# A two-block network on one core: the second expert table for 192 tokens as stationary blocks, for the last 64 tokens as gathered rows

## The chip, the core and the metric

The kernel runs on one core of a Trainium2 chip. The number that counts is the device time of one execution, in microseconds; the median of the runs is given. The engines are TensorE (PE, with its weight loads as PEld), VectorE (DVE), ScalarE (ACT), GpSimd (POOL) and SyncE (SP, which only issues DMAs here).

## What is computed

256 tokens of width 1024 go through two blocks: a block with an mLSTM mixer, an MLP and a gated embedding, then a block with two mixers and, at its end, an expert layer. Only this last layer is touched. Its reference, cut to what matters:

```python
q = (xb @ w_q).reshape(t, 8, 2, 128)
s = einsum('thpd,hpkd->thpk', q, sub_keys)
top_s, top_i = lax.top_k(s, 16)
cand_s = top_s[:, :, 0, :, None] + top_s[:, :, 1, None, :]
cand_i = top_i[:, :, 0, :, None] * 128 + top_i[:, :, 1, None, :]
best_s, best_pos = lax.top_k(cand_s.reshape(t, 8, 256), 16)
idx = take_along_axis(cand_i.reshape(t, 8, 256), best_pos, axis=-1)
gate = softmax(best_s, axis=-1)
h = gelu(einsum('thkd,td->thk', u_table[idx], xb))
y = einsum('thk,thkd->td', gate * h, v_table[idx])
x = layer_norm(DN_ALPHA * x + y)
```

Each token chooses 8 x 16 = 128 of 16384 experts; `u_table` and `v_table` have a row of 1024 for each.

## The kernel before

**Weights as a stream.** All weights are a list of 438 items of 128 x 1024 fp32 (512 KB). An item goes through a ring of four slots: SP loads it to `RAW` (wait `w_lo` of the item four before), ScalarE casts it to the high half `WH` (fp32r; waits `w_landed` and `w_used` of the item four before, counts `w_hi`), GpSimd or VectorE subtracts `RAW - WH` to the low half `WL` (counts `w_lo`), TensorE multiplies with high and low halves and counts `w_used`. A product is split in three: high x high, high x low, low x high.

**First table (`u`, 128 items).** No rows are chosen: for each item j, TensorE computes the products of 128 experts with all 256 tokens (24 matmuls of 256 columns, table blocks stationary), ScalarE applies gelu into `HS[:, j, :]` (128 partitions x 256 tokens). Low halves are GpSimd's (`split_low`, L398-L403). A round of four items is `u_body`.

**Gates.** VectorE finds the chosen experts; from `HOT_AT` = 15 on, one block of 16 tokens for each round, it writes one-hot rows (`one_hots`), TensorE turns them into a 128 x 128 table of gates for each token (`gates_of`, L1643), and VectorE multiplies the part j < `KEPT` = 60 into `HS` (`gate`). The rest is parked in DRAM (`gates_rest`) through `stage` and multiplied in during the second table (`fetch` on ScalarE's queue, `gate_rest` on VectorE).

**Second table (`v`, 128 items).** For item j, `HS[:, j, :]`, now gated, is the stationary operand, as high half `CH` (ScalarE, `c_high`) and low half `CL` (VectorE, `c_low`), and the table block with 1024 columns is moved past it: for both tiles of 128 tokens and both halves of 512 columns, three matmuls, so 12 of 512 columns (`v_item`, L1694). The sums stay in four banks of PSUM, tokens on the partitions. VectorE makes both low halves (`v_low`, `c_low`); GpSimd has nothing to do. The last four items are taken tile by tile, so that the first tile's layer norm runs beside the second tile's matmuls. All orders are written out in the code; every engine works through its own instructions strictly in that order.

## Time and profile before

| | us |
|---|---|
| median of 3 runs | 1406.85 |
| the 3 runs | 1406.48 to 1407.96 |
| span of the profiled execution | 1407.2 |

| engine | busy, us | share of the span |
|---|---|---|
| TensorE | 1379.8 | 98% |
| TensorE, weight loads | 1219.1 | 87% |
| VectorE | 889.0 | 63% |
| ScalarE | 869.5 | 62% |
| GpSimd | 763.7 | 54% |

The page gives the profiled execution by its span, from the first to the last instruction; it is 0.35 us above the median of the runs. The span falls into stages: up to about 690 us everything ahead of the tables, then the first table (with the gates in it from 829 us), the second table from 1051.47 us, and a last norm from 1399.85 us. Shares over the whole span mix these stages, so they are read one by one below. Busy times of matmuls overlap, since a matmul starts before the one ahead has drained; what a matmul costs is read from start to start.

### The profile page before, as it was taken

Reading aid. Unit: us, or ns where it says so; the run is one execution under the profiler, and the core shown is the slowest. Engines: PE = TensorE matmul, PEld = TensorE weight load, DVE = VectorE, ACT = ScalarE, POOL = GpSimd, SP = SyncE. Lnnn points to the kernel's source line nnn. Section 1 sums busy time; section 2 is a strip of 40 time slices with the busy share of each in tenths; the row PEclk is TensorE's granted clock in tenths of the full one; section 3 lists DMA queues with packets and bytes.
Section 4 is the critical chain, followed back from the end, with each engine's and each line's share of the span. In section 5 each row is a group of like instructions: output and inputs, shape, how many; then the busy total and the mean of one; then the engine's idle time right before and its main releaser. Section 6 shows DMA issues by size and latency. Waiting matters only on the chain.

```text
span 1407.2 us, 28597 instructions
## 1 busy us (share of the span) xinstructions
PE 1379.8 (98%) x9422; PEld 1219.1 (87%) x9422; DVE 889.0 (63%) x1967; ACT 869.5 (62%) x1496; POOL 763.7 (54%) x350
## 2 busy tenths in 40 slices
PE   7999999999999999899999999999999999999997
PEld 6878888887998777789999999999998888888886
DVE  3674883114764654535997059999977766655555
ACT  5475775446855656566666768888874444445553
POOL 6885889886776424687888877777740000000000
PEclk9999999999999999999999999999999999999999
DMA  5633566655453312655555556565669777666552
GB/s 199 204 133 120 183 194 199 188 194 165 147 163 125 122 61 85 199 195 165 190 173 190 180 174 201 196 202 191 201 200 324 272 241 241 210 194 193 192 192 94
DMA packets 75352, 256.63 MB, mean 182 GB/s; under 512 B 8472, under 2 KB 8856, under 8 KB 75032
## 3 DMA queue, kind: packets, MB, share of 16 engines
q1 hardware_dynamic: 64192, 231.76, 50.3%
q10 hardware_dynamic: 11096, 24.00, 5.0%
q8 instruction: 42, 0.69, 0.2%
q14 instruction: 22, 0.18, 0.1%
HBM read 244.72 MB, written 11.01 MB: 182 GB/s over the span
## 4 chain that ended last, share of the span: by engine, by line
PE 75%; POOL 12%; issue 8%; DVE 3%; DMA 1%; ACT 0%; POOLq 0%; ACTq 0%; DVEq 0%; SPq 0%
PE PS L1080 64%; POOL WL L402 11%; PE PS L1125 2%; PE PS L1643 2%; PE PS L1126 1%; PE PS L1462 1%; DMA RAW<-weights 0%; PE PS L1420 0%; DVE MINV L2167 0%; DVE GA L1810 0%; DMA fbias<-fox_bias 0%; DVE XS L2277 0%; DVE GA L1809 0%; PE PS L1619 0%; PE PS L1364 0%
## 5 line engine op out<-in xcount | busy, mean ns | idle before, releaser
L402 POOL TENSOR_TENSOR WL<-RAW,WH 128x1024 fp32r<-128x1024 f32 x306 | 739.4, 2427 | 270.5 <-ACT WH L461 182.6
L1080 PE MATMUL PS<-XHL,WH 128*128 128x256 f32 x2528 | 460.7, 284 | 2.4 <-DVE XHL L1763 1.5
L954 ACT CAST WH<-RAW 128x1024 fp32r<-128x1024 f32 x252 | 263.9, 1047 | 226.2 <-PE PS L1080 212.9
L1080 PEld LDWEIGHTS PS<-XHL,WH 128*128 128x128 f32 x2528 | 394.4, 192 | 5.9 <-issue 3.4
L1080 PE MATMUL PS<-XHL,WL 128*128 128x256 f32 x1264 | 357.7, 283 | 0.0
L461 ACT CAST WH<-RAW 128x1024 fp32r<-128x1024 f32 x184 | 191.3, 1047 | 108.9 <-PE PS L1080 95.8
L1080 PEld LDWEIGHTS PS<-XHL,WL 128*128 128x128 f32 x1264 | 242.6, 192 | 0.0
L2447 DVE TENSOR_TENSOR WL<-RAW,WH 128x1024 fp32r<-128x1024 f32 x128 | 156.6, 1224 | 116.9 <-ACT WH L954 116.2
L1080 PE MATMUL PS<-WH,CH 128*128 128x512 f32 x512 | 199.2, 389 | 0.0
L1080 PE MATMUL PS<-WL,CH 128*128 128x512 f32 x512 | 199.2, 389 | 0.0
L1080 PE MATMUL PS<-WH,CL 128*128 128x512 f32 x512 | 199.2, 389 | 0.0
L1125 PE MATMUL PS<-XHL,WH 128*128 128x512 f32 x384 | 138.3, 403 | 0.5 <-DVE XHL L2291 0.4
L1080 PE MATMUL PS<-WH,XHL 128*128 128x512 f32 x352 | 119.2, 403 | 1.2 <-POOL WL L402 1.2
L1080 PEld LDWEIGHTS PS<-WL,CH 128*128 128x128 f32 x512 | 96.1, 188 | 20.1
L1080 PEld LDWEIGHTS PS<-WH,CL 128*128 128x128 f32 x512 | 96.1, 188 | 19.9
L1080 PEld LDWEIGHTS PS<-WH,CH 128*128 128x128 f32 x512 | 96.1, 188 | 19.8
L930 ACT ACTIVATE hot_j<-hot_j,GQ 128x128 fp32r<-128x128 f32 x256 | 89.2, 395 | 33.7 <-DVE hot_j L2397 33.7
L1126 PE MATMUL PS<-XHL,WL 128*128 128x256 f32 x384 | 108.0, 281 | 0.0
L2397 DVE TENSOR_SCALAR hot_j<-PS,JT,GH 128x128 fp32r<-128x128 f32 x256 | 92.1, 401 | 0.0
L1125 PEld LDWEIGHTS PS<-XHL,WH 128*128 128x128 f32 x384 | 72.7, 189 | 18.2 <-issue 1.2
L1080 PEld LDWEIGHTS PS<-WH,XHL 128*128 128x128 f32 x352 | 66.6, 189 | 17.6 <-ACT og L579 1.2
L1126 PEld LDWEIGHTS PS<-XHL,WL 128*128 128x128 f32 x384 | 73.1, 190 | 0.0
(407 smaller groups left out, 1959.3 us busy)
## 6 DMA issues: line engine op xcount, KB each, us to landing
RAW<-weights SPq DMA_DIRECT2D x438, 512.0 KB, 3.5
gates_rest<-stage ACTq DMA_DIRECT2D x32, 272.0 KB, 2.2
stage<-gates_rest ACTq DMA_DIRECT2D x32, 272.0 KB, 4.2
H<-x SPq DMA_DIRECT2D x2, 512.0 KB, 4.7
LG<-rows ACTq DMA_DIRECT2D x2, 512.0 KB, 6.6
LB<-rows ACTq DMA_DIRECT2D x2, 512.0 KB, 8.9
x<-H ACTq DMA_DIRECT2D x1, 1024.0 KB, 6.1
HY<-x ACTq DMA_DIRECT2D x1, 1024.0 KB, 13.2
```

What stands on the lines that cost most here:

```text
L402: nc.gpsimd.tensor_tensor(WL[:, slot, :], RAW[:, slot, :], plain(WH[:, slot, :]), ALU.subtract).then_inc(w_lo, 1)
L461: nc.scalar.copy(high_of(n), RAW[:, slot, :]).then_inc(w_hi, 1)
L930: last = A(hot_j[:, g, a, 1, :], plain(hot_j[:, g, a, 0, :]), ACT.Copy, scale=at_token(GQ, t))
L954: nc.scalar.copy(WH[:, slot, :], RAW[:, slot, :]).then_inc(w_hi, 1)
L1080: last = mm(dst, a, b, start=start and k == 0, stop=stop and k == len(pairs) - 1)
L1125: mm(both, wh, XHL[:, :, k, :], start=(k == 0), stop=False)
L1126: last = mm(PS[:, bank, 0:S], wl, XH[:, k, :], start=False, stop=(k == KC - 1))
L1462: last = mm(product_of(half, h2, crossed)[:, u * CH_T:(u + 1) * CH_T], inv[a][rows, unit, :], right, start=True, stop=True)
L1643: last = mm(PS[:, 4 + 2 * (c % 2) + g, a * 2 * NK:(a + 1) * 2 * NK], hot_i[:, g, a, :], hot_j[:, g, a, :, :], start=True, stop=True)
L2397: last = V.tensor_scalar(hot_j[:, g, a, 0, :], iota_ps, at_token(JT, t + a), at_token(plain(GH), t + a), ALU.is_equal, ALU.mult)
L2447: V.tensor_tensor(WL[:, slot, :], RAW[:, slot, :], plain(WH[:, slot, :]), ALU.subtract).then_inc(w_lo, 1)
```

## The change

Of the 256 tokens, the last `TS` = 64 leave the dense way through the second table. `TD` = 192 stay in it.

- **192 tokens, table blocks stationary.** High and low halves of the gated hidden values stand side by side in `CHL` (2 x 192). For each of 8 chunks of 128 output columns, the high half of the table block is loaded and 384 columns (high and low) are moved past it, then the low half of the block, past which 192 are moved. The result has output columns on the partitions, one PSUM bank for each chunk. At the end ScalarE and VectorE add the two parts of a bank, and TensorE transposes back (`back`).
- **64 tokens, rows gathered.** For 64 steps, GpSimd gathers 128 rows of 1024 from the second table (`gather_row`, two experts of each of the 64 tokens, three buffers `rows_v`) and 128 hidden values (`gather_hidden`) by indirect DMA; VectorE multiplies each row by gate and hidden value and adds it up in `sparse_y` (`add_row`). TensorE folds the two groups of 64 partitions (`sparse_back`). The hidden values of these tokens are stored to DRAM (`hidden`) during the first table, by SP after each round, the last by ScalarE.
- **Low halves.** Every fourth low half of the second table is GpSimd's (`value_low`, counting `pool_lo`), three of four are VectorE's.
- **Gates** are made for 12 blocks of 16 tokens and not 16, so `HOT_AT` is 19; `KEPT` is 64.
- **The end.** The last four items are taken chunk by chunk once all four are ready; both tiles' norms come after them.
- **Semaphores** of earlier stages are used again (`LATER` maps a name to an old one and its last value), and the loops over the second table are written out without a loop on ScalarE, VectorE and GpSimd.

The diff, cut to its core:

```diff
-IJG_AT = NK // 8 - 2
-HOT_AT = NK // 8 - 1
-HOT_END = HOT_AT + S // 16
-KEPT = 4 * HOT_AT
+IJG_AT = NK // 8 - 2
+HOT_END = NK // 4 - 1
+HOT_AT = HOT_END - TD // 16
+KEPT = 64
+MAC_FROM, MAC_TO = 13, 119
+MAC_AT = [MAC_FROM + k * (MAC_TO - MAC_FROM) // STEPS for k in range(STEPS)]
+BATCH = STEPS // 8
...
 @block.gpsimd
+            def value_low(j):
+                slot = (V0 + j) % RING
+                pool.wait_ge(w_hi, V0 + j + 1)
+                nc.gpsimd.tensor_tensor(WL[:, slot, :], RAW[:, slot, :], plain(WH[:, slot, :]),
+                                        ALU.subtract).then_inc(sem("pool_lo"), 1)
+            def gather_row(k):
+                if k >= ROWS:
+                    pool.wait_ge(sem("row_added"), late_at("row_added", k - ROWS + 1))
+                nc.gpsimd.indirect_dma_start(
+                    out=rows_v[:, k % ROWS, :], out_offset=None, in_=expert_rows,
+                    in_offset=bass.IndirectOffsetOnAxis(ap=v_row[:, k:k + 1], axis=0)).then_inc(
+                        sem(f"row_landed{k % ROWS}"), 16)
...
+            for k in range(ROWS):
+                gather_row(k)
+            for q in range(NK // RING):
+                value_low(RING * q + RING - 1)
+                if q == 0:
+                    pool.wait_ge(sem("h_stored"), late_at("h_stored", 16 * (SELF_STORED + 1)))
+                for k in range(STEPS):
+                    if max(MAC_AT[k] - 20, 0) // RING == q:
...
+                        gather_hidden(k)
+                for k in range(STEPS):
+                    if MAC_AT[k] // RING == q and k + ROWS < STEPS:
+                        gather_row(k + ROWS)
...
 @block.tensor
-            def v_item(j, c, start=False, stop=False, tiles=range(NT)):
...
-                    for half in range(2):
-                        wh = WH[:, slot, half * 512:(half + 1) * 512]
-                        wl = WL[:, slot, half * 512:(half + 1) * 512]
-                        last = split([(h, wh), (h, wl), (l, wh)], PS[:, 2 * t + half, :], start, stop)
+            def v_chunk(c, ch, start=False, stop=False):
+                slot = (V0 + c) % RING
+                wh, wl = WH[:, slot, ch * P:(ch + 1) * P], WL[:, slot, ch * P:(ch + 1) * P]
+                mm(PS[:, ch, 0:2 * TD], wh, CHL[c][:, :, :].rearrange("p a t -> p (a t)"), start=start, stop=False)
+                return mm(PS[:, ch, 0:TD], wl, CHL[c][:, 0, :], start=False, stop=stop)
...
+            for c in range(RING):
+                item_ready(NK // 4 - 1, c)
...
+            for ch in range(KC):
+                for c in range(RING):
+                    last = v_chunk(c, ch, stop=(c == RING - 1))
+                last.then_inc(sem("chunk_done"), 1)
+                if ch >= 3:
+                    back(ch - 3)
...
 @block.vector
+            def add_row(k):
...
+                wait(f"row_landed{k % ROWS}", 16 * (k // ROWS + 1))
+                wait("row_added", late_at("row_added", k))
...
+                    V.scalar_tensor_tensor(sparse_y[:, :], rows_v[:, k % ROWS, :], h_s[:, k:k + 1], sparse_y[:, :],
+                                           ALU.mult, ALU.add).then_inc(sem("row_added"), 1)
...
+            for j in range(NK):
+                if j % RING < RING - 1:
+                    value_low(j)
+                c_low(j)
...
+                if rests < TD // 16 and (j in (5, 7, 9, 11) or j > 12 and j % RING == 1):
+                    for b in range(2):
+                        gate_rest(rests, b)
+                    rests += 1
+                for k in range(STEPS):
+                    if MAC_AT[k] == j:
+                        add_row(k)
...
-                layer_norm(1, t, [2 * t, 2 * t + 1], DN_ALPHA, LG2, LB2, 64, "y_ready")
+                layer_norm(1, t, [t, 2 + t], DN_ALPHA, LG2, LB2, 64, "y_ready")
```

What this does to the order of instructions. On VectorE, in the loop over the second table while parked gates are still fetched, before (`WL` is a low half, `CL` a remainder, `HS<-HS,stage` a gate multiply):

```order
L2447 TENSOR_TENSOR WL<-RAW,WH 128x1024 [waits w_hi]
L2424 REGISTER_ALU
L2426 ISA [waits ch_ready]
L2426 TENSOR_TENSOR CL_183<-HS,CH 128x256
L2418 ISA
L2420 ISA [waits fetched0]
L2420 TENSOR_TENSOR HS<-HS,stage 128x68x8
L2420 ISA [waits fetched1]
```

The same place now (items 17 to 19; `sparse_y` is the running sum of rows, and the semaphore named `s_ready` counts the adds):

```order
L2626 TENSOR_TENSOR WL<-RAW,WH 128x1024 [waits w_hi]
L2602 TENSOR_TENSOR CHL_186<-HS,CHL_186 128x192 [waits ch_ready]
L2597 TENSOR_TENSOR HS<-HS,stage 128x64x8 [waits fetched0]
L2597 TENSOR_TENSOR HS<-HS,stage 128x64x8 [waits fetched1]
L2640 SCALAR_TENSOR_TENSOR sparse_y<-rows_v,h_s,sparse_y 128x1024 [waits s_ready,row_landed0]
L2626 TENSOR_TENSOR WL<-RAW,WH 128x1024 [waits w_hi]
L2602 TENSOR_TENSOR CHL_187<-HS,CHL_187 128x192 [waits ch_ready]
L2602 TENSOR_TENSOR CHL_188<-HS,CHL_188 128x192 [waits ch_ready]
L2640 SCALAR_TENSOR_TENSOR sparse_y<-rows_v,h_s,sparse_y 128x1024 [waits s_ready,row_landed1]
```

Row adds stand among the low halves, and the fourth item of a round has a remainder but no low half. On GpSimd, the end of the program before (the last low halves of the first table, with nothing behind them):

```order
L402 TENSOR_TENSOR WL<-RAW,WH 128x1024 [waits w_hi]
L445 REGISTER_ALU
L445 COMPARE_AND_BRANCH
L402 TENSOR_TENSOR WL<-RAW,WH 128x1024 [waits w_hi] x2
L118 UNCONDITIONAL_BRANCH
```

And now, three rounds of four items in the second table (`rows_v` is a gather of rows, `h_s` one of hidden values):

```order
L529 TENSOR_TENSOR WL<-RAW,WH 128x1024 [waits w_hi]
L543 DMA h_s<-hidden,h_at 128x1 x2
L536 DMA rows_v<-weights,v_row 128x1024 [waits s_ready] x2
L529 TENSOR_TENSOR WL<-RAW,WH 128x1024 [waits w_hi]
L543 DMA h_s<-hidden,h_at 128x1 x2
L543 DMA h_s<-hidden,h_at 128x1 [waits s_ready]
L536 DMA rows_v<-weights,v_row 128x1024 [waits s_ready] x3
```

GpSimd goes on through the second table, with one low half and some five gathers for each round, each row gather behind an add of VectorE.

## Rows read from the trace of the kernel before

**Rows 1.** The page's busy line: busy us, share of the span, instructions.

```profile
PE 1379.8 (98%) x9422; PEld 1219.1 (87%) x9422; DVE 889.0 (63%) x1967; ACT 869.5 (62%) x1496; POOL 763.7 (54%) x350
```

**Rows 2.** Stages: length, busy by engine (instructions), granted clock, DMA share, GB/s.

```profile
829.15:1051.47 222.32, 222.32 (x1854) 222.13 (x1852) 208.64 (x573) 185.51 (x419) 153.99 (x64) 1.00 0.59 196
1051.47:1399.85 348.38, 348.35 (x1538) 288.20 (x1536) 221.07 (x296) 172.94 (x257) 0.00 (x0) 1.00 0.65 217
```

**Rows 3.** Chain of waits, late gates and second table: start, length, engine and line.

```profile
1034.35 0.48 PE PS L1643 x4
1034.83 2.88 PE PS L1080 x24
...
1041.55 358.28 PE PS L1080 x1620
```

**Rows 4.** Timeline of TensorE at key scores: start, length, line, names, weights, columns.

```profile
604.62 0.28 PE L1619 MATMUL PS<-KK,QH 128*128 128x256 f32 x1
604.74 0.23 PE L1620 MATMUL PS<-KK,QL 128*128 128x128 f32 x1
604.80 0.34 PE L1619 MATMUL PS<-KK,QH 128*128 128x256 f32 x1
604.98 0.22 PE L1620 MATMUL PS<-KK,QL 128*128 128x128 f32 x1
605.03 0.44 PE L1125 MATMUL PS<-XHL,WH 128*128 128x512 f32 x1
605.32 0.28 PE L1126 MATMUL PS<-XHL,WL 128*128 128x256 f32 x1
```

**Rows 5.** Timeline of ScalarE and VectorE in the second table, where VectorE is behind.

```profile
1083.10 1.05 ACT L954 CAST WH<-RAW 128x1024 fp32r<-128x1024 f32 x1
...
1084.40 1.39 DVE L2420 TENSOR_TENSOR HS<-HS,stage 128x544 f32 x2
1085.71 1.22 DVE L2447 TENSOR_TENSOR WL<-RAW,WH 128x1024 fp32r<-128x1024 f32 x1
1086.85 0.42 DVE L2426 TENSOR_TENSOR CL<-HS,CH 128x256 fp32r<-128x256 f32 x1
1087.18 1.22 DVE L2447 TENSOR_TENSOR WL<-RAW,WH 128x1024 fp32r<-128x1024 f32 x1
```

**Rows 6.** Timelines of GpSimd and VectorE, early; one line's shortest, median, longest ns.

```profile
149.78 2.41 POOL L402 TENSOR_TENSOR WL<-RAW,WH 128x1024 fp32r<-128x1024 f32 x1 [0.26 <-ACT WH L461]
...
150.53 0.42 DVE L1936 SCALAR_TENSOR_TENSOR RT<-PS,RB 128x256 f32<-128x256 f32 x1
150.87 1.59 DVE L1928 TENSOR_TENSOR ZL<-ZF,ZH 128x256 fp32r<-128x256 f32 x1
...
L1928 DVE TENSOR_TENSOR ZL<-ZF,ZH x32: 409/1578/1595, 142.9 to 226.8; 128x256 fp32r<-128x256 f32 x32
...
675.18 2.28 DVE L2344 TENSOR_TENSOR cand<-tv 128x2048 f32<-128x2048 f32 x1
...
675.59 6.51 POOL L402 TENSOR_TENSOR WL<-RAW,WH 128x1024 fp32r<-128x1024 f32 x2 [0.47 <-ACT WH L954]
```

**Rows 7.** Two short windows (columns as rows 2); DMA issues from 1060 to 1100.

```profile
1060.00:1070.00 10.00, 10.00 (x46) 8.29 (x45) 4.95 (x7) 4.06 (x6) 0.00 (x0) 1.00 1.02 414
1080.00:1090.00 10.00, 10.00 (x45) 8.28 (x45) 9.75 (x14) 5.45 (x9) 0.00 (x0) 1.00 0.92 285
...
RAW<-weights SPq DMA_DIRECT2D x14, 512.0 KB, 5.0
```

**Rows 8.** Timeline of the last norm on VectorE; six fp32 transposes in the chain.

```profile
1399.85 0.69 DVE L2270 SCALAR_TENSOR_TENSOR HY<-HY,PS 128x512 f32<-128x512 f32 x1 [0.47 <-PE PS L1080]
...
1401.44 1.28 DVE L2277 SCALAR_TENSOR_TENSOR XS<-HY,ST,LG 128x1024 f32<-128x1024 f32 x1
...
1403.34 1.42 DVE L2283 SCALAR_TENSOR_TENSOR HY<-XS,ST,LB 128x512 f32<-128x512 f32 x2
...
812.66 0.66 PE PS L1681 x6
```

More of the change, by code:

```diff
@@ L286, in sem @@
         def sem(name):
+            name = LATER[name][0] if name in LATER else name
             if name not in sems:
@@ L1040, in _ @@
[L1040 to L1043 removed]
+                if j >= 12 and j % RING == 0 and j // RING <= TD // 16 - 2:
+                    next_blocks(j // RING)
+                if j == 40:
+                    act.wait_ge(w_used, V0 + 32)
+                    act.wait_ge(sem("x2_stored"), 16)
+                    act.dma_start(LG2[:, :], rows_in[4:5, :].broadcast_to([P, D])).then_inc(sem("ln_landed"), 16)
+                    act.dma_start(LB2[:, :], rows_in[5:6, :].broadcast_to([P, D])).then_inc(sem("ln_landed"), 16)
+                    act.dma_start(HY[:, :, :].rearrange("p t d -> p (t d)"), x2_dram).then_inc(sem("x2_back"), 16)
@@ new lines, in _ @@
+            wait("u_bank_free", NK // 2)
+            for ch in range(2):
+                last = v_chunk(0, ch, start=True)
+            last.then_inc(w_used, 1)
+            for c in range(1, RING):
+                item_ready(0, c)
+                for ch in range(KC):
+                    last = v_chunk(c, ch)
+                last.then_inc(w_used, 1)
+            with pe.Fori(1, NK // 4 - 1) as i:
+                for c in range(RING):
+                    item_ready(i, c)
+                    for ch in range(KC):
+                        last = v_chunk(c, ch)
+                    last.then_inc(w_used, 1)
@@ new lines, in _, with back @@
+            for c in range(RING):
+                item_ready(NK // 4 - 1, c)
+            def back(ch):
+                wait("units_ready", late_at("units_ready", 1))
+                wait("chunk_summed", late_at("chunk_summed", max(ch + 1, 2 if ch < 4 else 4)))
+                g, k = ch // 4, slice(ch % 4 * P, ch % 4 * P + P)
+                first_tile = tp(PS[:, 2 * g, k], dense_y[:, ch, 0:P], unit[:, :])
+                second_tile = mm(PS[0:TD - P, 2 * g + 1, k], dense_y[:, ch, P:TD], unit[:, :], start=True, stop=True)
+                if ch == KC - 1:
+                    first_tile.then_inc(sem("tile_done"), 1)
+                    second_tile.then_inc(sem("tile_done"), 1)
@@ new lines, in sparse_back @@
+            def sparse_back(g):
+                wait("row_added", late_at("row_added", STEPS))
+                wait("chunk_summed", late_at("chunk_summed", 2 * g + 2))
+                mm(PS[P - TS:P, 2 * g + 1, :], group_sum[:, :], sparse_y[:, g * 512:(g + 1) * 512], start=True, stop=True)
+            for ch in range(KC):
+                for c in range(RING):
+                    last = v_chunk(c, ch, stop=(c == RING - 1))
+                last.then_inc(sem("chunk_done"), 1)
+                if ch >= 3:
+                    back(ch - 3)
+                if ch in (4, 6):
+                    sparse_back(ch // 2 - 2)
@@ L1720, in _ @@
+            for ch in range(KC - 3, KC):
+                back(ch)
         @block.vector
@@ L2440, in _ @@
                     gate(i, c - 1)
-            gate(S // 16 - 1, 3)
-            def v_low(j, c):
-                slot = (FIRST["v_table"] + c) % RING
-                dve.wait_ge(w_hi, j + (FIRST["v_table"] + 1))
-                V.tensor_tensor(WL[:, slot, :], RAW[:, slot, :], plain(WH[:, slot, :]), ALU.subtract).then_inc(w_lo, 1)
-            dve.wait_ge(w_lo, FIRST["v_table"])
-            for c in range(4):
-                v_low(c, c)
-                c_low(c, c)
-            wait("u_bank_free", NK // 2)
@@ L2473, in _, with value_low @@
-            for c in range(4):
-                low_halves(KEPT + c, c)
-            with dve.Fori(HOT_AT + 1, NK // 4) as i:
-                for c in range(4):
-                    v_low(4 * i + c, c)
-                    c_low(4 * i + c, c)
+            gate(TD // 16 - 1, 3)
+            V0 = FIRST["v_table"]
+            def value_low(j):
+                slot = (V0 + j) % RING
+                dve.wait_ge(w_hi, V0 + j + 1)
+                V.tensor_tensor(WL[:, slot, :], RAW[:, slot, :], plain(WH[:, slot, :]), ALU.subtract).then_inc(w_lo, 1)
@@ L2480, in _ @@
+            assert rests == TD // 16
+            for ch in range(KC):
+                wait("y_low_ready", late_at("y_low_ready", ch + 1))
+                V.tensor_tensor(dense_y[:, ch, :], PS[:, ch, 0:TD], y_low[:, ch % 2, :], ALU.add).then_inc(
+                    sem("chunk_summed"), 1)
             wait("x2_back", 16)
```

300 lines of the change are left out of this document (186 added, 114 removed).

## Prediction, made before the changed kernel ran

> **What bounds the kernel now.** I read the busy line first, then the table by stage, the chain, and last single instructions. TensorE is busy 98% of the span [rows 1], and in the three stages of the expert tables it has no gap at all, at a granted clock of 1.00 [rows 2]. The chain of waits agrees: from the end of the gates to 1399.83 us it is one unbroken piece of matmuls [rows 3]. So time is won there only by giving TensorE less to do, and only as long as the engines that feed it keep the new pace. The second-table stage (1051.47 to 1399.85, 348.4 us) is 1536 matmuls of 512 columns, 0.227 us each, 12 to a block: 2.72 us for each of the 128 blocks. Beside them VectorE is busy 221 us, ScalarE 173 us, GpSimd 0, and the DMA share is 0.65 [rows 2].
>
> **TensorE in the second table.** A block now takes, for each of 8 chunks, one matmul of 384 and one of 192 columns: 4608 columns, not 6144. Price of a matmul: 512 columns start 0.23 us apart (348.4/1536 = 0.227) and 256 columns 0.12 us (24 in 2.88 us) [rows 2, 3], so 0.107 us for each 256 columns and 0.013 us fixed. By that line 384 columns cost 0.174 and 192 cost 0.094 us: 8 x 0.268 = 2.14 us a block. The nearest rows to the short one speak against the line. Two pairs of 256 and 128 columns and then one of 512 take from 604.62 to 605.32, 0.70 us; less 2 x 0.12 and 0.235, the two of 128 columns cost 0.225, so 0.112 us each instead of the 0.067 of the line [rows 4]. Something of about 0.11 us between two loads of weights seems to be a floor. With 0.112 for the 192 columns a block is 8 x 0.286 = 2.29 us, and I take that. 128 blocks: 274 us by the line, 293 by the floor, against 348.
>
> The Trainium skill, TensorE: Matmul & The Clock Gate, "Back-to-back issue gap", gives about 81 ns for 128 columns in a stream of load and matmul pairs. The rows here show 112 ns for such a matmul, so the measurement decides; by the page's figure, as an estimate, there would be no floor at 192 columns, and the TensorE term would be the 274 us.
>
> **The gates in the first table.** Only 192 tokens get one-hot matmuls, so 12 of the 16 blocks of gates stay (HOT_AT moves from 15 to 19). One block is 4 groups of 0.48 us on a full TensorE [rows 3]: 4 blocks x 4 x 0.48 = 7.7 us saved. VectorE has 208.6 of 222.3 us in that stretch [rows 2]; its work for each block hardly changes (64 blocks kept in place rather than 60), so nothing new is late. The stores of the last 64 tokens' hidden values stand on SP behind loads that it has issued by then, and wait for evacuations some ten blocks old: nothing.
>
> **VectorE and GpSimd in the second table: the new limit.** The order lists show for each four blocks on VectorE three low halves, four coefficient remainders and two or three row adds, on GpSimd the fourth low half and some five gathers. Prices by start-to-start [rows 5]: a low half 1.14 us (1085.71 to 1086.85), a remainder of 256 columns 0.33 (1086.85 to 1087.18), so 0.27 for 192; a pair of gate multiplies of 544 1.31 (1084.40 to 1085.71), so 1.24 for a pair of 512. A row add is a scalar_tensor_tensor of 1024, which the trace has at 1.28 us [rows 8] where the low half has 1.22, so 1.20 start-to-start; the small multiplies of the gates come to 1 us in all. VectorE alone: 96 x 1.14 + 128 x 0.27 + 64 x 1.20 + 12 x 1.24 + 1 = 237 us, 1.85 us a block. By this alone TensorE would stay the bound.
>
> But the two engines do not run side by side on this work. At 150.87 VectorE starts ZL<-ZF,ZH, 256 columns with both inputs in SBUF, while GpSimd is inside a low half (149.78 for 2.41 us); it takes 1.59 us instead of 0.41 at its shortest and ends 0.27 us after GpSimd. RT<-PS,RB just before, with one input in PSUM, takes its 0.42 us inside the same GpSimd instruction. The other way round, GpSimd's low half of 675.59 has to sit out VectorE's 2.28 us: two of them take 6.51 us together [rows 6]. So a VectorE instruction with both inputs in SBUF and a GpSimd low half exclude one another. Before, GpSimd was idle in this stage; now 32 low halves of 2.4 us run there, and every VectorE instruction of the stage has both inputs in SBUF. The two add: 237 + 32 x 2.4 = 314 us. The quarter that was given to GpSimd thus costs VectorE 2.4 us a piece, where doing it itself would cost 1.14.
>
> Now in order of time, T0 being TensorE's first block. Blocks 0 to 12 have no adds: 13 x (0.86 + 0.27 + 0.6) + 5 pairs x 1.24 = 29 us on VectorE and GpSimd, 13 x 2.29 = 30 on TensorE: TensorE's pace, and VectorE, three blocks ahead, reaches block 13 at about T0 + 24. Blocks 13 to 118: 106 x 1.73 + 64 x 1.20 + 7 x 1.24 = 269 us, 2.53 us a block, above TensorE's 2.29. Where VectorE was behind in the trace it was busy 9.75 of 10 us [rows 7], so 276 us: T0 + 300. Then TensorE's pace for 6 blocks, 14 us. The last four blocks start only when all four low halves are there: after block 123 a cast (1.05 us [rows 5]) and GpSimd's 2.4 us: 3.5 us with TensorE idle, where the old code went on block by block. Then 4 x 2.29 = 9 us, and the transposes back: 16 at 0.11 us (0.66 us for 6 fp32 transposes [rows 8]) and two sums of 512 columns at four times that, 2.6 us; they are at most that, and nothing if they fit beside other waits. Sum: T0 + 329 instead of 348: **19 us saved**.
>
> **The end.** Both tiles' layer norms now come after the last matmul; before, the first ran beside the second tile's matmuls. One norm goes from 1399.85 to 1404.76, 4.9 us [rows 8]. The second adds these 4.9, and copy, add and transposes of the last chunk some 1.3: **6 us lost**.
>
> **Gathers.** The trace has no indirect DMA. 128 of them stand on GpSimd, half of 512 KB and half of 0.5 KB. No row is near; for the issue I take as the lower end nothing and as the upper end GpSimd's longest common instruction, one low half, 2.4 us. In 9.9 us (four blocks) GpSimd has 3.0 us for its low half with a wait, and 4.9 gathers: it fits up to 1.4 us each. I take about 1 us, so hidden, and keep both ends. The Trainium skill, DMA: Bandwidth & Descriptors, "Latency and other measured facts", puts about 1 us before the first byte of a DMA generated on GpSimd; at that estimate the 128 would be 128 us of GpSimd, and the sum would not change. No run shows it yet.
>
> **The sum.** 1407.2 (span) - 7.7 - 19 + 6 = 1386.5; the median lies 0.35 us under the span, so **1386 us**. Own range 1372 (no floor at 192 columns, no idle in VectorE's queue) to 1400 (a few us at the start, where the first four row gathers and the wait for the stores precede GpSimd's first low halves).
>
> **Rivals.** (a) *TensorE stays the bound*: the exclusion does not bite, because the low half on GpSimd slips into VectorE's gaps. Then 274 to 293 us of matmuls + 3.5 + 2.6: 280 to 299, so 49 to 68 saved in the stage, 1337 to 1357. For it: the remaining VectorE load of 1.85 us a block. Against: VectorE has no gaps long enough, by the sum above.
>
> (b) *The DMA engines saturate.* The stage moves 67 MB of table and now 34 MB of gathered rows and 6 MB of gates, 107 MB. At 414 GB/s, the best ten microseconds (share 1.02), that is 258 us and hidden; at 285 GB/s for a share of 0.92 [rows 7], 310 at full share, it is 345 us, as long as the stage was. Then the stage gains nothing but the gates' 7.7 us are kept and the end's 6 are lost: 1395 to 1415, about no change. 4 KB rows from random places are read like the table's rows, which speaks against the worse figure.
>
> (c) *Rows arrive late, and it becomes slower.* A row's gather stands on GpSimd behind the low half of its group, and that waits for a cast, which waits for TensorE to give the slot free. Take the row for block 21: block 15 on TensorE 2.3, cast 1.2, GpSimd's low half 3.0, two small gathers and one large, then the landing, 5 us in the busiest stretch [rows 7]; VectorE comes to block 21 six blocks after block 15, 15 us later. So three issues have 3.7 us, 1.2 each; beyond that VectorE waits in its queue with low halves behind the add, and TensorE behind them. At 2 us an issue it is 2.3 us late in each of some 26 groups, +60 us: 1446. The point where the gain is gone: 21 us / 26 groups, 0.8 us late in each, an issue of 1.5 us. For it: three buffers of rows and a strictly ordered queue. Also here: GpSimd holding the port while it makes descriptors, 64 x 1 us or more.
>
> **Chances.** Forecast 0.48, (a) 0.12, (b) 0.14, (c) 0.26. Faster by over 0.2% (about 3 us, what a measurement of this kernel can tell from no change): 0.47 + 0.12 + 0.05 = 0.64; within 0.2%: 0.01 + 0.04 + 0.02 = 0.07; slower: 0.05 + 0.24 = 0.29. The range leaves out the low end of (a) and the upper part of (c): 1345 to 1450.
>
> **What would show it.** In the changed kernel's profile: pairs of 384 and 192 columns 0.27 to 0.29 us apart; VectorE close to 100% in blocks 13 to 118, its low halves stretched to some 3 us about once in four blocks; TensorE's waits there ending with VectorE's or GpSimd's low half; a gap of about 3.5 us ahead of the last four blocks; two norms in a row at the end. Rival (a): no TensorE gap before the last group. (b): ScalarE's casts waiting for RAW. (c): row adds waiting for the gather. It is wrong if the low halves on GpSimd do not stretch VectorE's instructions, or if a gather holds GpSimd for longer than 1.4 us.

## Result: slower, and the profile after

The median is 1441.51 us (1440.85 to 1453.14) against 1406.66 us for the kernel before: a ratio of 1.0263 (95% interval 1.0246 to 1.0280), 35 us slower. The forecast was 1386 us; the time lies inside the range, on the other side of no change, near rival (c). The busy line of the profiled execution (span 1439.9 us; engine, us, share, instructions) answers to [rows 1]:

```profile
PE 1351.2 (94%) x9898; PEld 1241.8 (86%) x9898; DVE 914.6 (64%) x1870; ACT 837.8 (58%) x1424; POOL 999.9 (69%) x516
```

TensorE's share fell from 98% to 94% although it has less to do. The table by stage (stretch, length, busy time and instructions of PE, PEld, DVE, ACT and POOL, granted clock, DMA share, GB/s) answers to [rows 2]; the second table now begins at 1041.1 us, and the transposes back follow its last matmul at 1425.2:

```profile
829.15:1041.05 211.90, 211.75 (x1754) 210.73 (x1753) 159.52 (x435) 158.57 (x339) 150.01 (x63) 1.00 0.63 200
1041.05:1426.90 385.85, 329.20 (x2075) 320.81 (x2074) 286.28 (x326) 166.12 (x261) 235.73 (x164) 0.91 0.78 278
```

The first line is what was hoped for: TensorE full, 10.4 us gained by the fewer gates. The second is the loss: 386 us where the stage before had 348. No engine is full in it, VectorE has 286 of 386 us, and the granted clock is 0.91 where it was 1.00, since TensorE now stops again and again. What each waited for, 1045 to 1405 us (engine, line and tile, releaser; us in total, times, longest):

```profile
ACT WH L1106 <- DMA RAW<-weights: 115.4, 49, 8.0
POOL WL L529 <- ACT WH L1106: 84.9, 24, 10.2
ACT WH L1106 <- PE PS L1831: 79.4, 52, 6.3
DVE sparse_y L2640 <- DMA rows_v<-weights,v_row: 55.0, 20, 7.6
PEld PS L1830 <- DVE CHL L2602: 53.2, 19, 6.7
```

Everybody waits for everybody: ScalarE for weights and for TensorE, GpSimd for ScalarE, TensorE for VectorE. Only the fourth line is new in kind: the row adds wait for gathered rows. GpSimd's groups in 1045 to 1385 us (line, engine, operation, tiles, count; busy us, mean ns; idle before):

```profile
L543 POOL DMA_INDIRECT h_s<-hidden,h_at x64 | 77.4, 1209 | 15.7 <-issue 13.9
L536 POOL DMA_INDIRECT rows_v<-weights,v_row x63 | 75.3, 1196 | 23.5 <-issue 15.6 <-DVE sparse_y L2640 7.4
L529 POOL TENSOR_TENSOR WL<-RAW,WH 128x1024 fp32r<-128x1024 f32 x30 | 74.9, 2497 | 74.8 <-ACT WH L1106 74.7
```

A gather holds GpSimd for 1.2 us on the mean, a small one as long as a large one, and 0.3 us lie between two in a row: 1.5 us. Over all 127 of these two lines, with the idle time put down to "issue", it is 1.43 us each. The Trainium skill, DMA: Bandwidth & Descriptors, "Latency and other measured facts", has about 1 us to the first byte of such a DMA. No row here shows a first byte; for GpSimd's own time the measured 1.5 us decides. Now one wait in order of time, first GpSimd, then VectorE (start, us, instruction; idle before it and what ended it):

```profile
1176.44 2.39 POOL L529 TENSOR_TENSOR WL<-RAW,WH 128x1024 fp32r<-128x1024 f32 x1 [2.23 <-ACT WH L1106]
1178.99 1.77 POOL L543 DMA_INDIRECT h_s<-hidden,h_at  x1
1181.07 1.38 POOL L543 DMA_INDIRECT h_s<-hidden,h_at  x1 [0.30 <-issue]
1182.75 1.09 POOL L543 DMA_INDIRECT h_s<-hidden,h_at  x1 [0.30 <-issue]
1184.15 1.10 POOL L536 DMA_INDIRECT rows_v<-weights,v_row  x1 [0.30 <-issue]
```
```profile
1170.99 1.27 DVE L2640 SCALAR_TENSOR_TENSOR sparse_y<-rows_v,h_s,sparse_y 128x1024 f32<-128x1024 f32 x1
...
1176.45 3.47 DVE L2640 SCALAR_TENSOR_TENSOR sparse_y<-rows_v,h_s,sparse_y 128x1024 f32<-128x1024 f32 x1 [0.94 <-DMA rows_v<-weights,v_row]
...
1184.08 0.35 DVE L2602 TENSOR_TENSOR CHL<-HS,CHL 128x192 fp32r<-128x192 f32 x1
1191.08 1.28 DVE L2640 SCALAR_TENSOR_TENSOR sparse_y<-rows_v,h_s,sparse_y 128x1024 f32<-128x1024 f32 x1 [6.65 <-DMA rows_v<-weights,v_row]
```

The cast ended at 1176.37. Behind it stand the low half, three gathers of hidden values, and only at 1184.15 the row that VectorE wants: it lands near 1191, and for 6.65 us VectorE stands with all later low halves behind the add. The buffer for that row had long been free: the add three rows earlier (1170.99) ended at 1172.26, so its gather started 11.9 us late. Over all rows a gather starts a mean of 4.9 us after its buffer is free (start of each row's gather less the end of the add three rows before, from the two timelines).

Rows land a median 7.4 us after their issue, and weights now take 6.2 us and not 3.5 (lines of the DMA issues; the kernel before over its whole span, where its second table alone has 3.5 too, then the changed kernel, 1070 to 1380 us):

```profile
RAW<-weights SPq DMA_DIRECT2D x438, 512.0 KB, 3.5
```
```profile
RAW<-weights SPq DMA_DIRECT2D x105, 512.0 KB, 6.2
rows_v<-weights,v_row POOLq DMA_INDIRECT x61, 7.4
```

### The profile page after: what moved, and what is told of

Read it like the earlier page. It is cut to its first block, busy times and chain, and to the rows that moved or that the text cites. A ratio compares the mean times of both kernels' runs of the same rounds, so it can differ in the third digit from the quotient of the medians.

```text
span 1439.9 us, 28703 instructions
## 1 busy us (share of the span) xinstructions
PE 1351.2 (94%) x9898; PEld 1241.8 (86%) x9898; DVE 914.6 (64%) x1870; ACT 837.8 (58%) x1424; POOL 999.9 (69%) x516
## 4 chain that ended last, share of the span: by engine, by line
PE 55%; POOL 16%; issue 10%; DMA 8%; DVE 8%; ACT 2%; ACTq 0%; POOLq 0%; DVEq 0%; SPq 0%
PE PS L1204 37%; POOL WL L472 11%; PE PS L1830 5%; DMA rows_v<-weights,v_row 5%; POOL WL L529 2%; PE PS L1249 2%; POOL h_s L543 2%; PE PS L1831 2%; DMA RAW<-weights 2%; PE PS L1767 2%; DVE sparse_y L2640 1%; ACT WH L1106 1%; DMA stage<-gates_rest 1%; PE PS L1250 1%; PE PS L1586 1%
## 5 line engine op out<-in xcount | busy, mean ns | idle before, releaser
L472 POOL TENSOR_TENSOR WL<-RAW,WH 128x1024 fp32r<-128x1024 f32 x306 | 739.5, 2427 | 259.5 <-ACT WH L583 177.9
L1830 PE MATMUL PS<-CHL,WH 128*128 128x384 f32 x1024 | 322.3, 384 | 56.7 <-DVE CHL L2602 52.7
L1831 PE MATMUL PS<-CHL,WL 128*128 128x192 f32 x1024 | 267.8, 262 | 0.0
L1830 PEld LDWEIGHTS PS<-CHL,WH 128*128 128x128 f32 x1024 | 207.6, 203 | 63.7 <-DVE CHL L2602 53.2
L1106 ACT CAST WH<-RAW 128x1024 fp32r<-128x1024 f32 x128 | 134.4, 1050 | 206.8 <-DMA RAW<-weights 115.4
L1204 PEld LDWEIGHTS PS<-XHL,WL 128*128 128x128 f32 x1264 | 242.4, 192 | 0.0
L1831 PEld LDWEIGHTS PS<-CHL,WL 128*128 128x128 f32 x1024 | 210.8, 206 | 0.0
L529 POOL TENSOR_TENSOR WL<-RAW,WH 128x1024 fp32r<-128x1024 f32 x32 | 79.6, 2489 | 91.7 <-ACT WH L1106 91.6
L2640 DVE SCALAR_TENSOR_TENSOR sparse_y<-rows_v,h_s,sparse_y 128x1024 f32<-128x1024 f32 x63 | 91.8, 1458 | 63.8 <-DMA rows_v<-weights,v_row 55.0
L2626 DVE TENSOR_TENSOR WL<-RAW,WH 128x1024 fp32r<-128x1024 f32 x96 | 122.7, 1278 | 9.7 <-ACT WH L1106 8.8
L536 POOL DMA_INDIRECT rows_v<-weights,v_row x64 | 76.9, 1201 | 31.7 <-issue 15.6
L543 POOL DMA_INDIRECT h_s<-hidden,h_at x64 | 77.4, 1209 | 15.7 <-issue 13.9
```

The lines of the kernel that those rows point to most:

```text
L472: nc.gpsimd.tensor_tensor(WL[:, slot, :], RAW[:, slot, :], plain(WH[:, slot, :]), ALU.subtract).then_inc(w_lo, 1)
L529: nc.gpsimd.tensor_tensor(WL[:, slot, :], RAW[:, slot, :], plain(WH[:, slot, :]), ALU.subtract).then_inc(sem("pool_lo"), 1)
L1106: nc.scalar.copy(WH[:, slot, :], RAW[:, slot, :]).then_inc(w_hi, 1)
L1204: last = mm(dst, a, b, start=start and k == 0, stop=stop and k == len(pairs) - 1)
L1830: mm(PS[:, ch, 0:2 * TD], wh, CHL[c][:, :, :].rearrange("p a t -> p (a t)"), start=start, stop=False)
L1831: return mm(PS[:, ch, 0:TD], wl, CHL[c][:, 0, :], start=False, stop=stop)
```

## The experiments

The expectations speak of four theories. **Theory 1**: the rows' traffic makes weights late, and a ring of four slots can't hide that. **Theory 2**: the exclusion of GpSimd's low halves and VectorE alone sets the pace (the forecast's own mechanism, larger than I had it). **Theory 3**: rows are late because their gather stands in GpSimd's queue behind a low half, so behind a cast, and behind small gathers (rival (c)). **Theory 4**, found on the way: VectorE's unbroken runs hold up the gathers. All runs, in the order of the text, against the kernel before:

| run | us | ratio, 95% interval |
|---|---|---|
| changed kernel | 1441.5 | 1.0263 (1.0246 to 1.0280) |
| a_short_rows | 1427.2 | 1.0144 (1.0127 to 1.0162) |
| b_dve_lows | 1422.6 | 1.0094 (1.0059 to 1.0129) |
| c_both | 1402.1 | 0.9969 (0.9950 to 0.9989) |
| d_short_adds | 1419.2 | 1.0073 (1.0053 to 1.0094) |
| h_no_gathers | 1387.1 | 0.9857 (0.9836 to 0.9879) |
| e_early | 1392.4 | 0.9895 (0.9871 to 0.9918) |
| f_stt | 1391.5 | 0.9889 (0.9867 to 0.9910) |
| g_seven | 1388.4 | 0.9855 (0.9831 to 0.9879) |
| k_ahead | 1413.4 | 1.0045 (1.0027 to 1.0063) |
| n_ahead_short | 1415.6 | 1.0051 (1.0031 to 1.0072) |
| p_no_hidden | 1426.5 | 1.0135 (1.0118 to 1.0153) |
| j_early_short | 1385.3 | 0.9845 (0.9828 to 0.9861) |
| l_tuned | 1379.5 | 0.9801 (0.9755 to 0.9846) |
| m_tuned32 | 1386.2 | 0.9848 (0.9831 to 0.9864) |

**a_short_rows.** Row gathers fetch 64 bytes of 4096.

```diff
-                    out=rows_v[:, k % ROWS, :], out_offset=None, in_=expert_rows,
+                    out=rows_v[:, k % ROWS, 0:D if k < ROWS else 16], out_offset=None, in_=expert_rows if k < ROWS else short_rows,
...
```

> All from the changed kernel; from the fourth gather on only 16 of the 1024 columns of each gathered row are fetched (the rest of the buffer keeps older rows, so the sums of the last 64 tokens are not those of the reference). Number of gathers, their issues, waits and the row adds stay: only some 32 MB of row traffic are gone. Theory 1, the rows' traffic makes the weights late (landing of a weight item 6.2 us instead of 3.5, in a ring of four slots): landing of RAW back to 3.4 to 3.8 us, ScalarE's waits for RAW (115 us) below 30 us, and the time falls by 40 us or more, to 1380 to 1400, where the sum of VectorE and GpSimd's low halves would set the pace. Theory 2, GpSimd's low halves and VectorE's instructions exclude each other and that alone sets the pace: 1430 to 1442, almost nothing. Theory 3, the gathers are issued too late behind GpSimd's other work: the issues stay, so most of the 55 us of row adds waiting stays, 1420 to 1440.

1427.2 us. Weights landed in 3.8 us again and the row gathers in 4.0, yet only 14 us came back, much as the third theory said: in this order of GpSimd's queue the traffic is not the main thing.

**b_dve_lows.** VectorE makes every low half.

```diff
-                nc.gpsimd.tensor_tensor(WL[:, slot, :], RAW[:, slot, :], plain(WH[:, slot, :]),
-                                        ALU.subtract).then_inc(sem("pool_lo"), 1)
...
-                if j % RING < RING - 1:
-                    value_low(j)
+                value_low(j)
```

> All from the changed kernel; the fourth low half of each four blocks is made by VectorE in the same place, GpSimd keeps its wait and its gathers. Theory 1 (weights late by the rows' traffic): the way of a slot from landing to free is 1.2 us shorter for one slot in four, and the traffic stays: 1415 to 1435, with RAW still landing after 6 us. Theory 2 (exclusion sets the pace): VectorE has 32 x 1.14 us more and loses 32 x 2.4 us of exclusion, so about 40 us less, 1390 to 1405 or lower. Theory 3 (late gathers): GpSimd has 77 us more for gathers, so the rows come earlier, 1400 to 1420.

1422.6 us, 19 us less: inside theory 1's span, just above theory 3's, and theory 2 is missed. The exclusion is gone (remainders are back at a mean of 352 ns, from 518), but the row adds still wait 51 us for their gathers, which stand behind the wait for the cast that GpSimd keeps.

```profile
L2639 DVE SCALAR_TENSOR_TENSOR sparse_y<-rows_v,h_s,sparse_y 128x1024 f32<-128x1024 f32 x63 | 80.8, 1283 | 54.8 <-DMA rows_v<-weights,v_row 51.0
```

**c_both.** Both edits.

> Both edits at once: 16 columns of each gathered row (from the fourth gather on; the last 64 tokens' sums are not the reference's) and all low halves on VectorE. Nothing is left but TensorE's 2.29 us a block if the two causes are all there is: stage of 293 us plus the end, 1345 to 1360. If the small gathers' issue (1.4 us each, start to start) or VectorE's 273 us with its waits is still late: 1360 to 1390.

1402.1 us, worse than every expectation. With no traffic and no exclusion, row adds still wait 34.8 us for gathered rows. So neither was the core of it. Some gathers last three times as long as others; GpSimd, then VectorE in the same stretch:

```profile
1134.19 2.51 POOL L542 DMA_INDIRECT h_s<-hidden,h_at  x1 [2.96 <-ACT WH L1105]
1137.00 3.70 POOL L542 DMA_INDIRECT h_s<-hidden,h_at  x1 [0.30 <-issue]
```
```profile
1137.00 1.22 DVE L2626 TENSOR_TENSOR WL<-RAW,WH 128x1024 fp32r<-128x1024 f32 x1
1138.13 0.35 DVE L2602 TENSOR_TENSOR CHL<-HS,CHL 128x192 fp32r<-128x192 f32 x1
1138.40 1.21 DVE L2626 TENSOR_TENSOR WL<-RAW,WH 128x1024 fp32r<-128x1024 f32 x1
1139.54 0.35 DVE L2602 TENSOR_TENSOR CHL<-HS,CHL 128x192 fp32r<-128x192 f32 x1
1139.81 1.27 DVE L2641 SCALAR_TENSOR_TENSOR sparse_y<-rows_v,h_s,sparse_y 128x1024 f32<-128x1024 f32 x1
1141.00 1.21 DVE L2626 TENSOR_TENSOR WL<-RAW,WH 128x1024 fp32r<-128x1024 f32 x1
```

The gather of 1137.00 starts with a run of VectorE's low halves and ends at 1140.70, 0.9 us into a row add. 32 of the 128 gathers last over 1.8 us here, and all 32 begin while VectorE is busy; the 20 that begin beside an idle VectorE last 0.94 or 0.95 us each. The first of the two starts only when a cast ends: the queue's order.

**d_short_adds.** Whole gathers, adds of 16 columns.

> All from the changed kernel; rows are gathered whole, but the row add takes 16 of 1024 columns (the last 64 tokens' sums are not the reference's). VectorE has some 70 us less to do, everything else stays. Theory 1 (weights late by the traffic): VectorE is not what is late, 1425 to 1442. Theory 2 (VectorE plus excluded low halves set the pace): 1375 to 1395. Theory 3 (late gathers): a wait for a row stays as it is, 1425 to 1442.

1419.2 us: 70 us less on VectorE gave 22. More than the first and third theories allowed, far less than the second. The adds waited 90.7 us for rows now, from 55: the rows come when GpSimd sends them.

**h_no_gathers.** Nothing is gathered; each gather is a write of a fraction of a microsecond on GpSimd.

```diff
-                nc.gpsimd.indirect_dma_start(out=rows_v[:, k % ROWS, :], ...
+                nc.gpsimd.memset(rows_v[:, k, :] if k < ROWS else v_row[:, k:k + 1], 0).then_inc(
+                    sem(f"row_landed{k % ROWS}"), 16)
...
-                nc.gpsimd.indirect_dma_start(out=h_s[:, k:k + 1], ...
+                nc.gpsimd.memset(h_s[:, k:k + 1], 0.0).then_inc(sem(f"h_landed{k // BATCH % 2}"), 16)
```

> From the changed kernel, with GpSimd's low halves kept; the 64 row gathers and 64 gathers of hidden values are replaced by a small write on GpSimd each, so nothing is gathered (the last 64 tokens get no expert sum); waits, counts and the 64 whole row adds on VectorE stay. It is the sum of the prediction without its gathers. If that sum was right (VectorE and GpSimd's low halves exclude each other and add up to 2.53 us a block) and the miss is all in the gathers: 1375 to 1395. If the exclusion costs more than the sum says: 1405 to 1430. If the exclusion hardly counts and TensorE's 2.29 us a block are the bound: 1345 to 1365.

1387.1 us, the forecast's 1386. Its stretch with adds in every group, 1100 to 1340 us (columns as in the table by stage), and three groups there:

```profile
1100.00:1340.00 240.00, 228.67 (x1560) 223.97 (x1559) 237.91 (x248) 125.57 (x193) 96.24 (x124) 0.99 0.72 231
```
```profile
L2635 DVE SCALAR_TENSOR_TENSOR sparse_y<-rows_v,h_s,sparse_y 128x1024 f32<-128x1024 f32 x58 | 110.4, 1904 | 0.2
L2621 DVE TENSOR_TENSOR WL<-RAW,WH 128x1024 fp32r<-128x1024 f32 x74 | 93.9, 1268 | 1.8 <-ACT WH L1101 1.8
L529 POOL TENSOR_TENSOR WL<-RAW,WH 128x1024 fp32r<-128x1024 f32 x24 | 90.8, 3784 | 101.0 <-ACT WH L1101 101.0
```

VectorE is busy 237.9 of 240 us, row adds are stretched from 1.28 to a mean of 1.90 us and GpSimd's low halves from 2.4 to 3.78: the exclusion, the full VectorE and its size are as foretold. All of the miss, 54 us, is the gathers, with everything that hangs on them.

Its second table to the transposes back answers to the 385.85 us of the changed kernel:

```profile
1040.70:1371.00 330.30, 310.28 (x2085) 301.28 (x2084) 305.35 (x327) 166.85 (x262) 122.22 (x164) 0.98 0.68 223
```

For as many matmuls the changed kernel takes 56 us more. In 37 of these TensorE stands (56.7 us in all, here 20.0); in 19 it is busy longer, at a granted clock of 0.91 on the mean where it is 0.98 here. Its waits cost a second time through the clock; how much of the 19 us would be hidden otherwise is not shown.

**e_early.** As b_dve_lows, and GpSimd's queue holds gathers alone, each issued when its buffer is free.

```diff
-            for q in range(NK // RING):
-                value_low(RING * q + RING - 1)
...
+            for k in range(2 * BATCH):
+                gather_hidden(k)
+            for k in range(ROWS, STEPS):
+                gather_row(k)
+                if k + 2 * BATCH - ROWS < STEPS:
+                    gather_hidden(k + 2 * BATCH - ROWS)
```

> All low halves on VectorE as in b_dve_lows, and GpSimd's gathers no longer stand behind casts: each row gather is issued as soon as its buffer is free (three rows earlier added), hidden values 13 rows ahead. Theory 3 (rows late because of GpSimd's queue): a row has 3 adds' spacing, some 11 us, for one or two issues and 7.5 us of landing, so most of the 51 us of row adds waiting goes: 1395 to 1410, against 1422. Theory 1 alone (traffic makes the weights late): 1415 to 1425, as b_dve_lows.

1392.4 us, 3 us under theory 3's span and 30 us under b_dve_lows with the same work and the same traffic: the order of GpSimd's queue and the wait for the cast in it, theory 3. A row's gather now starts a mean of 0.7 us after its buffer is free, and the row adds' 51.0 us of waiting for rows are 4.0:

```profile
L2627 DVE SCALAR_TENSOR_TENSOR sparse_y<-rows_v,h_s,sparse_y 128x1024 f32<-128x1024 f32 x63 | 80.6, 1279 | 4.2 <-DMA rows_v<-weights,v_row 4.0
```

The DMA engines now move 345 GB/s on the mean and ScalarE's 130 us of waiting for weights are in 92 pieces of at most 4.3 us (in the changed kernel 115.4 us in 49, at most 8.0).

**f_stt.** Low halves and remainders as scalar_tensor_tensor.

```diff
-                V.tensor_tensor(WL[:, slot, :], RAW[:, slot, :], plain(WH[:, slot, :]), ALU.subtract).then_inc(
+                V.scalar_tensor_tensor(WL[:, slot, :], RAW[:, slot, :], 1.0, plain(WH[:, slot, :]),
+                                       ALU.mult, ALU.subtract).then_inc(
```

> As e_early, and VectorE's low halves and remainders are written as scalar_tensor_tensor (times 1.0, minus) instead of tensor_tensor. In c_both gathers that begin in a run of tensor_tensor lasted up to 4.9 us and ended some 0.9 us after a scalar_tensor_tensor began or VectorE went idle. Theory 4, the runs of tensor_tensor hold GpSimd's gathers: the longest gather falls to 2 us or less, and the time is 5 to 20 us under e_early, although VectorE pays some 0.06 us more for each low half (8 us in all). Against it: the gathers keep their length and the time is the 8 us longer.

1391.5 us, no difference to e_early, and the gathers are no shorter: 19 of 128 over 1.8 us (11 in e_early), the longest 4.58 us. That the instruction's kind lets gathers pass is refuted. That gathers last longer inside VectorE's unbroken runs stands; what ends such a wait is open, and what it costs in time no run shows.

**g_seven.** Four more row buffers.

```diff
-ROWS = 3
+ROWS = 7
-MAC_FROM, MAC_TO = 13, 119
+MAC_FROM, MAC_TO = 20, 124
-        rows_v = at("rows_v", [P, ROWS, D], F32, 8448)
+        rows_v = [at(f"rows_v{k}", [P, D], F32, 8448 + 4096 * k if k < 3 else A0 + 4096 * (k - 3)) for k in range(ROWS)]
```

> As f_stt, with seven row buffers instead of three (four lie in the room of the hidden values of blocks 0 to 15, from block 16 on) and the adds moved to blocks 20 to 123. Rows are asked for seven adds, some 26 us, ahead. Theory 3: row adds wait less than 5 us in all, and the time is 1365 to 1390; what remains is weights that land late (theory 1) in the ring of four. If theory 1 is most of the loss: 1395 to 1415 with ScalarE's waits for RAW still over 100 us.

1388.4 us: no row add waits on the list any more, and only 3 us are won against f_stt, on which it is built, at the edge of what the two can tell apart. ScalarE waits 131.8 us for weights, as theory 1 said, which does not say yet that it costs.

**k_ahead.** The changed kernel with GpSimd's order alone changed.

```diff
+                for k in range(STEPS):
+                    if MAC_AT[k] // RING == q and MAC_AT[k] % RING < 2 and k + ROWS < STEPS:
+                        gather_row(k + ROWS)
                 value_low(RING * q + RING - 1)
...
```

> The changed kernel with GpSimd's order alone changed: of each group the row gathers whose buffer is freed in the first two blocks stand ahead of the group's low half, all row gathers stand ahead of the hidden gathers. Work, traffic and engines are as in the changed kernel. Theory 3 (the row is late because its gather stands behind the low half and so behind the cast): row adds wait less than half of their 55 us and the time is 1405 to 1425. Theory 1 (traffic alone): 1435 to 1442. It can't be under h_no_gathers, 1387. Against it: GpSimd then waits for an add with a low half queued behind, which could give the gain back.

1413.4 us, 28 of the 54 us. A row's gather starts 2.1 us after its buffer is free (mean; 4.9 in the changed kernel), the row adds' wait is gone, and a new one is there (1045 to 1385 us: the group of row adds, then a wait of TensorE):

```profile
L2643 DVE SCALAR_TENSOR_TENSOR sparse_y<-rows_v,h_s,sparse_y 128x1024 f32<-128x1024 f32 x63 | 92.6, 1470 | 2.8 <-DMA rows_v<-weights,v_row 2.6
```
```profile
PE PS L1833 <- POOL WL L529: 19.5, 11, 4.7
```

TensorE waits 19.5 us for GpSimd's low halves (3.9 in the changed kernel): they now stand behind the gathers.

**n_ahead_short.** k_ahead with 64 bytes a row, for the 26 us left over h_no_gathers.

> k_ahead (GpSimd's order alone changed) with 16 columns of each gathered row from the fourth gather on (the last 64 tokens' sums are not the reference's). Between k_ahead (1413) and h_no_gathers (1387) 26 us are left. Theory 1, they are the rows' traffic, by which a weight item lands late: 1385 to 1395, ScalarE's waits for RAW down from 137 us to near 107 us, h_no_gathers' value, or below. Rival: they are the gathers on GpSimd, which keep its low half waiting: 1405 to 1413.

1415.6 us, not below k_ahead and 3 us over the rival's span: the traffic is not what is left there. TensorE's wait for GpSimd's low halves is 31.8 us. So the rival is left, the gathers' time on GpSimd ahead of its low halves; this wait speaks for it, and no run takes that time away alone.

**p_no_hidden.** The changed kernel without the small gathers.

> The changed kernel without the 64 gathers of hidden values (a small write in the place of each, so the last 64 tokens get no expert sum); row gathers whole, order as in the changed kernel. GpSimd's queue loses 64 x 1.45 = 93 us, the traffic stays. Theory 3 (a row is late because of what stands ahead of it on GpSimd: the low half and two hidden gathers): 1405 to 1425. Theory 1 (traffic): 1432 to 1442.

1426.5 us, 15 us less, 1.5 us over theory 3's span and under theory 1's: 64 gathers of 0.5 KB cost about as much as the traffic of the 64 large ones (a_short_rows, 14). GpSimd now has room, 182 us busy of 340 (columns as in the table by stage), and the row adds still wait:

```profile
1045.00:1385.00 340.00, 301.36 (x1975) 294.72 (x1974) 290.05 (x314) 160.37 (x250) 181.73 (x163) 0.96 0.87 315
```
```profile
DVE sparse_y L2637 <- DMA rows_v<-weights,v_row: 24.9, 14, 4.3
```

39 us over h_no_gathers stay; how they divide between the queue's order, the landing of rows and the traffic is not shown.

**j_early_short.** e_early with 64 bytes a row.

> e_early (all low halves on VectorE, gathers issued as soon as a buffer is free) with 16 columns of each gathered row from the fourth gather on (the last 64 tokens' sums are not the reference's). In e_early the DMA share is 0.96 on the mean and ScalarE waits 130 us for weights. Theory 1 as what is left (the DMA engines are full): without some 32 MB of rows TensorE's 2.29 us a block set the pace, 1350 to 1370. If instead VectorE's 273 us with its waits are what is left: 1380 to 1392.

1385.3 us: once nothing stands in GpSimd's way, the whole traffic is worth 7 us. From 1180 to 1340 us TensorE has no gap (one stretch of 20 us below); what it loses lies ahead of that, in gaps of the first forty blocks or so, among them waits for parked gates (10 us on VectorE, 13 on ScalarE behind it).

```profile
1140.00:1160.00 20.00, 16.52 (x113) 15.82 (x111) 15.64 (x22) 6.44 (x10) 14.87 (x13) 1.00 0.87 307
...
1240.00:1260.00 20.00, 20.00 (x143) 20.00 (x142) 19.05 (x24) 11.25 (x19) 14.57 (x11) 1.00 0.75 233
```

**l_tuned.** All low halves on VectorE, early gathers, seven buffers, and the edits below.

```diff
-                if rests < TD // 16 and (j in (5, 7, 9, 11) or j > 12 and j % RING == 1):
+                if rests < TD // 16 and j >= 5 and j % RING == 1:
...
-                if j == 40:
+                if j == 108:
...
-                for c in range(RING):
+                for c in range(2, RING):
                     last = v_chunk(c, ch, stop=(c == RING - 1))
```

> A version meant to be best: all low halves on VectorE (tensor_tensor), early gathers, seven row buffers with adds in blocks 20 to 123, the parked gates fetched every four blocks and not two, the 2 MB for the last norm loaded at block 108 and not 40, and of the last four blocks only two taken chunk by chunk. Theory 1 as what is left: 107 MB at 350 GB/s are 306 us from 1041 us on, and 14 us of end: 1361 at best, 1362 to 1382 with the waits; no better than g_seven (1388) if VectorE is what is left.

1379.5 us, 28 us under the kernel before in the same series (1407.6). Whole rows run at TensorE's pace from 1200 to 1300 us with the DMA engines full:

```profile
1220.00:1240.00 20.00, 20.00 (x143) 20.00 (x142) 18.34 (x25) 11.34 (x18) 16.04 (x14) 1.00 1.03 400
```

**m_tuned32.** The same for 32 tokens.

```diff
-TS = 64
+TS = 32
```

> l_tuned with 32 tokens in rows and 224 in the dense way (half the gathers and adds, 90 MB instead of 107). TensorE: 8 x (0.20 + 0.107) = 2.46 us a block, 315 us from 1045 us on, and 14 us of end: 1374. If the DMA engines are what is left of l_tuned, this one is on TensorE's pace with no gaps, 1370 to 1380.

1386.2 us: TensorE is full in every stretch from 1060 to 1360 us, at the price worked out (130 matmuls in 20 us, 0.154 us each, 2.46 a block), and is done 12 us later than I worked out, mostly by the end of the stage (below).

```profile
1200.00:1220.00 20.00, 20.00 (x130) 19.11 (x129) 14.44 (x18) 10.58 (x17) 6.42 (x6) 1.00 0.81 288
```

## Why the prediction was wrong

**The step that failed is the one on the gathers**: "it fits up to 1.4 us each. I take about 1 us, so hidden". The sum put them at nothing, and they cost 54 us (h_no_gathers). Their size was too low, with nothing near in the trace: 1.5 us in a row, 1.43 on the mean, large and small. But the size alone is not the loss: 1.43 is hardly over 1.4, and with half of the gathers gone GpSimd has room and 39 of the 54 us are still there (p_no_hidden). The test itself was the wrong one: that the gathers fit into GpSimd's time does not say when a row's gather has its turn in a strictly ordered queue. The runs show two ways to lose by it. First, the row's gather stands behind a cast, a low half and small gathers, and VectorE waits for it with its low halves queued behind: 28 us (k_ahead). Second, when the gathers go first, GpSimd's low halves are late for TensorE; with them on VectorE and a queue of gathers alone it is 1392 (e_early), a step that takes the exclusion away too, so its 21 us aren't all this. This second way is argued from the waits and from n_ahead_short, and no run shows its price.

**Rival (c) is what happened**, by the mechanism it names. Its price needs two sizes of the changed kernel: three issues of 1.5 us and a landing of 7.4 and not 5.0 us make 4.5 + 2.4 - 3.7 = 3.2 us late in each of 26 groups, 83 us; measured were 54. For p_no_hidden (one issue of 1.8 us, a landing of 7.7) the same sum gives some 20 us, and it lies 39 above h_no_gathers. So the mechanism and the sign hold and the price doesn't. What (c) adds, that GpSimd keeps VectorE out while it makes descriptors, did not come: VectorE's low halves take 1.22 us beside a gather and without one (c_both). I had given (c) 0.26; with the issue bounded only by 0 and 2.4 us and the threshold at 1.4, four in ten of that span lay beyond it. The range reached to 1450 on its account.

**Right, and shown by h_no_gathers (1387.1 for 1386):** the exclusion of GpSimd's low half and VectorE's instructions with both inputs in SBUF; VectorE near 100% (99%), though it is its row adds that are stretched (1.90 us) and not, as foretold, its low halves (1.27). TensorE's pairs of 384 and 192 columns are 0.28 us apart (143 matmuls in 20 us, l_tuned) where the line had 0.268 and the floor 0.286. The Trainium skill, GPSIMD Engine Reference, "Key points", names contention of GpSimd with VectorE's instructions that have two SBUF inputs; this trace agrees, with the 1.90 and 3.78 us above. The gap ahead of the last four blocks is 3.91 us for 3.5 (h_no_gathers, TensorE), and the two norms came in a row.

```profile
1353.83 0.66 PE L1825 MATMUL PS<-CHL,WH 128*128 128x384 f32 x1 [3.91 <-DVE CHL L2597]
```

**Mis-sized:** the end. The last four blocks and the transposes take 17.3 us in h_no_gathers (1353.83 to the start of the last chunk's transposes at 1371.1), not 9 + 2.6. The transposes back are fp32 products of 128 columns at 0.62 us a chunk (the last ones of the changed kernel below, start to start), 5.0 us for eight, with 2.1 us for the sums of the rows: 7.1, not 2.6. And the matmuls after the gap run slow (the changed kernel's table by stretch, one line each before the gap, in it and after it):

```profile
1425.78 0.33 PE L1859 MATMUL PS<-unit,dense_y 128*128 128x128 f32 x1
1426.04 0.43 PE L1860 MATMUL PS<-unit,dense_y 128*64 128x128 f32 x2
1426.40 0.33 PE L1859 MATMUL PS<-unit,dense_y 128*128 128x128 f32 x1
```
```profile
1400.00:1405.00 5.00, 5.00 (x37) 5.00 (x37) 3.73 (x6) 2.66 (x5) 0.00 (x0) 1.00 0.33 105
1405.00:1410.00 5.00, 1.09 (x6) 0.88 (x5) 3.23 (x3) 1.30 (x2) 2.34 (x1) 0.84 0.00 0
1410.00:1415.00 5.00, 5.00 (x21) 5.00 (x20) 0.72 (x2) 0.64 (x2) 0.00 (x0) 0.50 0.00 0
```

After 3.9 us without a matmul the granted clock is 0.50, the lower of its two levels (1.2 GHz), for the next 5 us: 21 matmuls and not 37, some 2 us. That the sum came out in h_no_gathers to 1 us is luck in part: the blocks ahead of the gap went some 5 us faster than the 2.53 us each of the sum, and the gates were worth 10.4 us by the start of the stage, not 7.7.

**Rivals (a) and (b).** (a) did not come: without gathers VectorE is full. (b), the DMA engines as the bound, is a small part: without the traffic 14 us come back in the changed kernel's own order, where rows then land sooner (a_short_rows), none once the rows are asked for in time (n_ahead_short), and 7 us where GpSimd has only gathers (j_early_short against e_early).

## What to carry to other kernels

Count an engine that issues indirect DMAs like one that computes: here 128 gathers of 1.43 us and 32 low halves of 2.5 us made some 263 us on GpSimd, in order, with waits among them. That fitted into the stage, and still the rows came late: ask of a queue when each piece has its turn, not only whether all of it fits. Where a price that no row shows decides the sign, the chances go by how much of its possible span lies beyond the threshold, not by one picked value. Don't let a prefetch stand behind work that waits for the present: the same gathers, asked for as soon as a buffer is free, made the kernel 30 us faster (e_early against b_dve_lows). And a small gather costs its issuer as much as a large one.
